# Last group of the SSM stage: which projections are products of parts, and where the rests of x are taken

## The chip, the cores and the metric

One core of a Trainium2 chip. The metric is the device time of one launch in microseconds (us). The engines are TensorE (PE, with its weight loads as PEld), VectorE (DVE), ScalarE (ACT), GpSimd (POOL) and SyncE (SP, which only issues transfers here).

## The reference, cut to what matters

The kernel is one step of a hybrid decoder layer on 544 tokens (512 of a prompt and 32 of eight samples). All branches begin with one projection of x:

```
cq, ckv_raw, kr_raw, z, xbc, dt_raw, mq, g_raw = split(x @ w_in)
# branch B (SSM), four groups of 8 heads of 64, chunks of 128 tokens
xbc -> causal conv -> silu -> xs, B, C
per chunk:  w = (C.B) * exp(cum_i - cum_j) * dt ;  y = w @ xs + (C @ S) * exp(cum)
            S = S * exp(last) + B^T (wb * xs)
y = (y + d_skip * xs) * silu(z) ; RMS norm over each group
# branch A (latent attention)
ckv = rms_norm(ckv_raw) ; krope = rope(kr_raw) ; q = rms_norm(cq) @ w_uq ...
```

A group of the SSM stage needs its 4 blocks of z (128 columns of w_in each) and computes, beside them, 6 blocks of something else: the conv inputs of the next group, or, in the last group, the latents (3 of cq, 2 of ckv, 1 of kr). These 6 are called "ahead".

## The kernel before, in words

Activations lie with features on the 128 partitions and the 544 tokens in the free dimension: x is 8 chunks (KC) of 128 features. A projection is one weight block of 128x1024 against x: for each half of the tokens (272 columns) 8 products, one for each chunk. There are two forms. The plain form (`project`, L1893) multiplies float32 by float32; the trace shows each such product as two records. The form of products of parts (`project_split`, L1908) multiplies rounded parts (type fp32r): x = XH + XL and w = high + low, and each chunk takes three products: high by XH, high by XL, low by XH. So a plain projection has 32 records and a split one 48.

The parts come from other engines. ACT rounds a weight block into one of three buffers (`round_head_block`, L774), DVE subtracts and leaves the rest in the block's own ring slot (`rest_of_head_block`, L1395, tile `ring_parts`). ACT rounds x into XH in group 2 (L779); DVE takes the rests XL (`rest_of_chunks`, L1389, tile `x_low`). `x_low` lies where `xt` lies: a chunk's rest overwrites the chunk, so DVE may take it only when the last plain product has read that chunk (semaphore `x_read`).

The stage runs a loop over 4 groups, with each engine's order written out by hand. TensorE: `project_x(1)`; sums of the last group; transposes of x and B (`turn`); `project_x(0)`, `project_x(1)` with the B by C products within, `project_x(0)` with the chunk states within (L2124). These four are z. Then `read_out(0)` (L2141 and L2147, two heads), `project_x(1)` with `sample_off` (L2157) within, `read_out(1)`, and five more projections with the samples' products and `read_out(2)`, `read_out(3)` between. `read_out(h)` waits for the two decay tiles that DVE has weighed (`weigh`, L1458) and for C scaled by GpSimd (`scale_c`, L515). After `sample_off` GpSimd scales four blocks of the samples' states (L521), two more C, and four more blocks. The split projection waits for `split_ready` of its block.

In groups 0 to 2 all ten projections are plain, in group 3 all ten are split. At the end of group 2 DVE takes the eight rests of x and the rest of the first split block, and only then runs the conv of the last ahead block (L1328 to L1342). ACT rounds ten blocks: two in the end of group 2, eight in group 3. `round_head_block(i)` waits, for i of 3 and more, until the block that used the same buffer has been read (`blocks_begun`). The ring has four slots that SP fills in order.

Of the kernel before, what the change touches and what calls it, by code (L numbers as in the profile page):

```python
# [3 lines left out]
P = 128  # L4
# [174 lines left out]
def program(nc, stream, x_t, mem_t, const, vec, conv_state, ssm_state, pages, ckv_rows, page_cols,  # L179
# [7 lines left out]
    with ExitStack() as ctx:  # L187
# [539 lines left out]
        def _(act):  # L727
# [130 lines left out]
            for g in range(GROUPS):  # L858
# [35 lines left out]
                if last_group:  # L894
                    round_head_block(3)
                if g:
# [262 lines left out]
        def _(dve):  # L1159
# [254 lines left out]
            for g in range(GROUPS):  # L1414
# [8 lines left out]
                rest_in_last_group(1)  # L1423

                def turned(*cs):
# [34 lines left out]
                z_gate(0)  # L1460
                rest_in_last_group(2)
                turned(2, 3)
# [9 lines left out]
                z_gate(1)  # L1472
                rest_in_last_group(3)
                dve.wait_ge(sem["rows_s_loaded"], t.next("rows_s_loaded", 16))
# [20 lines left out]
                weigh(1)  # L1495
                rest_in_last_group(4)
                z_gate(2)
# [6 lines left out]
                weigh(3)  # L1504
                rest_in_last_group(5)

# [43 lines left out]
                weigh(5)  # L1550
                rest_in_last_group(6)
                read_y(1)
                rest_in_last_group(7)
                ahead(1, between=read_y_s)
# [8 lines left out]
                add_state(1)  # L1563
                rest_in_last_group(8)
                ahead(2)
# [5 lines left out]
                gate_y(2)  # L1571
                rest_in_last_group(9)
                add_state(4)
# [9 lines left out]
                ahead_finish(3)  # L1583
                if g == GROUPS - 2:
                    for c in range(KC):
                        if c < KC - 1:
                            dve.wait_ge(sem["x_read"], c + 1)
                        else:
                            dve.wait_ge(sem["acc0_ready"], 4 + 5 * (GROUPS - 1))
# [283 lines left out]
        def _(pe):  # L1873
# [8 lines left out]

            def project(p, x, n_blocks=1, width=HT, between=None, read=None):

                pe.wait_ge(sem[f"acc{p}_free"], t.next(f"acc{p}_free"))
                for b in range(n_blocks):
                    w = next_block()
                    for half in range(2):
                        if half and between:
                            between()  # L1890
                        for k in range(KC):
                            kk = b * KC + k
                            m = pe.matmul(acc[p][:, half, 0:width], w[:, k * P:(k + 1) * P],  # L1893
                                          x(kk)[:, half * width:(half + 1) * width],
                                          start=kk == 0, stop=kk == n_blocks * KC - 1)
                            if half == 0 and k == 0:
                                m.then_inc(sem["blocks_begun"], 1)
                            elif half and read and k < KC - 1:
                                m.then_inc(sem[read], 1)
                m.then_inc(sem[f"acc{p}_ready"], 1)  # L1900
# [171 lines left out]
            for g in range(GROUPS):  # L2072
                B, C_ = bc[g % 2][:, 0, :], bc[g % 2][:, 1, :]
                def project_x(p, between=None, first=False, last=False):
                    if g == GROUPS - 1:
                        project_split(p, between, "low_even" if first else None)
                    else:
                        project(p, of_x, between=between, read="x_read" if last and g == GROUPS - 2 else None)

                project_x(1, first=True)  # L2080
                if g:
# [34 lines left out]

                project_x(1, between=b_by_c)
                pe.wait_ge(sem["b_tm_read"], t.next("b_tm_read"))
# [8 lines left out]
                states(0, 1)  # L2127
                project_x(0, between=lambda: states(2, 3))

# [55 lines left out]
                read_out(0)  # L2185
                project_x(1, between=sample_off)
                read_out(1)
                project_x(0)
                sample_y()
                project_x(1, between=lambda: state_adds(0))  # L2190
                read_out(2)
                state_adds(2)
                project_x(0, between=lambda: state_adds(4))
                read_out(3)
                project_x(1, between=lambda: state_adds(6))
                project_x(0, last=True)

# [431 lines left out]
```

## Time and profile before

| | |
|---|---|
| median of 3 runs | 1671.23 us (1668.9 to 1674.76) |
| profiled execution, its own time | 1669.8 us |
| its span | 1668.1 us |
| mean granted clock | 0.99 |
| PE busy | 1612.6 us, 97% |
| PEld busy | 1410.7 us, 85% |
| DVE busy | 797.4 us, 48% |
| ACT busy | 463.4 us, 28% |
| POOL busy | 411.1 us, 25% |

All times in the profile are from the span's start. A row of a timeline is: start, length, engine, line, operation, output tile and input tiles, their shapes, how many like it were merged, and in brackets the idle time before it with what ended it. Matmuls overlap in the records, so the pace is the distance of starts, not the length.

### The profile page before, as it was taken

The numbers are of one execution on the slowest core, as the hardware profiler recorded it, in microseconds if no ns is written. First come the engines' busy times: TensorE is split into PE (matmuls) and PEld (weight loads), VectorE is DVE, ScalarE is ACT, GpSimd is POOL, SyncE is SP. The second block draws the span as 40 slices with busy tenths as digits, with TensorE's granted clock in tenths as the row PEclk, the third lists the DMA queues.
The fourth block names the chain that finished last, engine by engine and source line by source line (L and its number), as shares of the span: only waits on it lengthen the run. The fifth ranks groups of instructions, "written<-read, shape, count | busy, mean of one in ns | idle before, by whom it ended". The sixth has DMA issues, their size and how long they took to land.

```text
span 1668.1 us, 27396 instructions
## 1 busy us (share of the span) xinstructions
PE 1612.6 (97%) x11110; PEld 1410.7 (85%) x11110; DVE 797.4 (48%) x1360; ACT 463.4 (28%) x867; POOL 411.1 (25%) x344
## 2 busy tenths in 40 slices
PE   8999999989999999999999999999989999999995
PEld 6878787768988888888888877789978999999995
DVE  5658676677533222223333223254488751177234
ACT  2252433526432222222122111142234111111122
POOL 0041131403320000001244200124444333344432
PEclk9999999999999999999999999999999999999998
DMA  5424334243462222224788766423322233222211
GB/s 179 136 81 165 95 110 144 76 155 108 140 231 66 74 76 76 64 78 152 254 270 270 250 260 245 160 89 89 102 64 64 89 89 89 89 89 84 86 59 54
DMA packets 71857, 210.67 MB, mean 126 GB/s; under 512 B 10321, under 2 KB 26962, under 8 KB 66866
## 3 DMA queue, kind: packets, MB, share of 16 engines
q1 hardware_dynamic: 51968, 157.04, 29.7%
q10 hardware_dynamic: 13618, 30.89, 5.2%
q0 software_dynamic: 6144, 20.98, 3.5%
q8 instruction: 88, 1.44, 0.4%
q14 instruction: 39, 0.32, 0.1%
HBM read 194.01 MB, written 14.86 MB: 125 GB/s over the span
## 4 chain that ended last, share of the span: by engine, by line
PE 82%; DVE 9%; ACTq 3%; ACT 3%; issue 2%; DMA 1%; SPq 0%; POOL 0%; DVEq 0%
PE acc L1962 30%; PE acc L1893 16%; PE acc L1908 12%; PE acc L2274 4%; PE acc L2237 3%; PE acc L2220 2%; ACTq L1053 1%; ACTq L1051 1%; DVE work L1342 1%; PE bank L2288 1%; PE bank L2307 1%; PE bank L2289 1%; DVE ring_parts L1395 1%; PE bank L2360 1%; PE bank L2392 1%
## 5 line engine op out<-in xcount | busy, mean ns | idle before, releaser
L1893 PE MATMUL acc<-xt,ring 128*128 128x272 f32 x1184 | 282.3, 395 | 0.0
L1893 PEld LDWEIGHTS acc<-xt,ring 128*128 128x128 f32 x1184 | 222.3, 190 | 53.1 <-issue 9.3
L1962 PE MATMUL acc<-x_parts,f_parts 128*128 128x272 f32 x1408 | 219.6, 291 | 10.6 <-DVE x_parts L1269 6.1
L565 POOL TENSOR_TENSOR f_parts<-ring,f_parts 128x1024 fp32r<-128x1024 f32 x65 | 157.9, 2429 | 247.9 <-ACT f_parts L789 247.6
L1962 PEld LDWEIGHTS acc<-x_parts,f_parts 128*128 128x128 f32 x1408 | 196.0, 191 | 13.3 <-issue 6.0
L543 POOL DMA_DIRECT2D work<-in_page_cols x128 | 68.9, 539 | 420.7 <-PE bank L2328 383.9
L1962 PE MATMUL acc<-f_parts 128*128 128x272 f32 x1344 | 172.3, 289 | 0.0
L1962 PEld LDWEIGHTS acc<-f_parts 128*128 128x128 f32 x1344 | 170.4, 188 | 0.1
L1908 PE MATMUL acc<-x_low,high 128*128 128x272 f32 x480 | 138.0, 288 | 0.0
L1908 PE MATMUL acc<-work_high,ring_parts 128*128 128x272 f32 x468 | 135.6, 290 | 0.0
L789 ACT ACTIVATE f_parts<-ring 128x1024 fp32r<-128x1024 f32 x65 | 69.0, 1061 | 238.9 <-PE acc L1962 204.5
L1908 PE MATMUL acc<-work_high,high 128*128 128x272 f32 x428 | 124.5, 291 | 0.0
L1395 DVE TENSOR_TENSOR ring_parts<-ring,high 128x1024 fp32r<-128x1024 f32 x38 | 48.4, 1274 | 90.4 <-ACT high L774 90.1
L1908 PEld LDWEIGHTS acc<-x_low,high 128*128 128x128 f32 x480 | 90.9, 189 | 0.4 <-issue 0.2
L1908 PEld LDWEIGHTS acc<-work_high,ring_parts 128*128 128x128 f32 x468 | 89.5, 191 | 0.0
L1908 PEld LDWEIGHTS acc<-work_high,high 128*128 128x128 f32 x428 | 80.4, 188 | 0.0
L1856 DVE TENSOR_SCALAR f_parts<-attended 128x544 fp32r<-128x544 f32 x32 | 76.2, 2383 | 1.1
L1342 DVE SCALAR_TENSOR_TENSOR work<-work,vecs 128x600 f32<-128x600 f32 x72 | 68.5, 951 | 2.4
L1962 PE MATMUL acc<-f_parts,mg_parts 128*128 128x272 f32 x528 | 68.8, 289 | 0.0
L565 POOL TENSOR_TENSOR mg_parts<-ring,mg_parts 128x1024 fp32r<-128x1024 f32 x21 | 50.8, 2417 | 71.1 <-ACT mg_parts L789 71.1
L1962 PEld LDWEIGHTS acc<-f_parts,mg_parts 128*128 128x128 f32 x528 | 67.3, 188 | 0.2
L1962 PE MATMUL acc<-x_parts,mg_parts 128*128 128x272 f32 x480 | 62.1, 289 | 0.6 <-DVE attended L1850 0.6
(385 smaller groups left out, 2738.7 us busy)
## 6 DMA issues: line engine op xcount, KB each, us to landing
ring<-in_stream SPq DMA_DIRECT2D x216, 512.0 KB, 3.6
work<-in_page_cols POOLq DMA_DIRECT2D x128, 160.0 KB, 5.2
attended<-in_ssm_state ACTq DMA_DIRECT2D x8, 1024.0 KB, 7.0
work<-cum_rows SPq DMA_DIRECT2D x32, 256.0 KB, 4.5
out_ssm_s<-attended ACTq DMA_DIRECT2D x8, 1024.0 KB, 5.7
work<-in_ckv_rows ACTq DMA_DIRECT2D x64, 128.0 KB, 3.6
work<-in_ckv_rows SPq DMA_DIRECT2D x64, 128.0 KB, 2.7
work<-in_memk_cols SPq DMA_DIRECT2D x8, 1024.0 KB, 7.1
```

The source lines that it names most:

```text
L543: pool.dma_start(keys[kq][:, i * KEYS_W:(i + 1) * KEYS_W], page_cols[ids[kq * 4 + i]]).then_inc(sem[f"keys_in_slot{kq}"], 16)
L565: pool.tensor_tensor(lo, ring[:, s * BLOCK:(s + 1) * BLOCK], hi.bitcast(F), SUB).then_inc(sem["split_ready"], 1)
L789: act.activation(hi, ring[:, s * BLOCK:(s + 1) * BLOCK], ACT.Copy).then_inc(sem["hi_ready"], 1)
L1342: dve.scalar_tensor_tensor(out=c, in0=ext[j][:, i:i + CL], scalar=tap(i), in1=c, op0=MUL, op1=ADD).then_inc(sem[signal], 1)
L1395: dve.tensor_tensor(ring_parts[:, of], ring[:, of], w_high_of(i).bitcast(F), SUB).then_inc(sem["split_ready"], 1)
L1856: dve.tensor_scalar(hi, q, 1.0, None, MUL).then_inc(sem["dve_step"], 1)
L1893: m = pe.matmul(acc[p][:, half, 0:width], w[:, k * P:(k + 1) * P], x(kk)[:, half * width:(half + 1) * width], start=kk == 0, stop=kk == n_ ...
L1908: m = pe.matmul(out[:, half, 0:HT], w[:, k * P:(k + 1) * P], x[k][:, of], start=k == 0 and n == 0, stop=last and k == KC - 1 and n == 2)
L1962: m = pe.matmul(acc_half, w[:, k * P:(k + 1) * P], x[:, kk, of], start=kk == 0 and n == 0, stop=kk == last and n == 2)
L2220: m = pe.matmul(acc[p][:, 0, 0:N_MEM], w[:, k * P:(k + 1) * P], mem[:, k, :], start=k == 0, stop=k == KC - 1)
L2237: m = pe.matmul(acc[p][:, half, 0:HT], w[:, c * 256 + off:c * 256 + off + P], cq[:, c, half * HT:(half + 1) * HT], start=c == 0, stop=c == 2)
L2274: m = pe.matmul(acc[1][:, half, 0:HT], w[:, k * P:(k + 1) * P], BR[:, KC + k, half * HT:(half + 1) * HT], start=False, stop=k == KC - 1)
```

## The change

In group 3 the four z projections become plain; the six latent ones stay split. The blocks that ACT and DVE split are numbered from the first latent block, so four rounds and four rests of weight blocks go. The fourth z projection runs chunk by chunk, both halves of a chunk together, and frees each chunk of x as it goes. DVE takes the eight rests of x in group 3, after `weigh(3)`. The first latent projection runs its products with XH first (two for each chunk, both halves, `sample_off` between), and then, chunk by chunk behind DVE, its products with XL. The end of group 2 has no rests and no rounds of weight blocks left.

```diff
-GROUP_SPLIT = GC + QC
+GROUP_SPLIT = QC
 # ACT, group 3
-                    round_head_block(2)          # after silu(0)
-                    round_head_block(3)          # after z_read(0)
                 z_read(1)
-                    round_head_block(4)
+                    round_head_block(0)
                 z_read(2)
-                    round_head_block(5)
+                    round_head_block(1)
                 ...
                 z_read(3)
-                    round_head_block(6)
+                    round_head_block(2)
                 # ahead(q)
-                    if g == GROUPS - 2 and q in (3, 4):
-                        round_head_block(q - 3)
-                        round_head_block(7 + q)
+                        round_head_block(3 + q)
 # DVE, group 3 (rest_in_last_group 1, 2, 3 before: gone)
                 weigh(0)
                 weigh(1)
-                rest_in_last_group(4)
+                rest_in_last_group(0)
                 ...
                 weigh(2)
                 weigh(3)
-                rest_in_last_group(5)
+                if g == GROUPS - 1:
+                    for c in range(KC):
+                        if c < KC - 1:
+                            dve.wait_ge(sem["x_read"], c + 1)
+                        else:
+                            dve.wait_ge(sem["acc0_ready"], 4 + 5 * (GROUPS - 1) + 2)
+                        rest_of_chunks(XL, X, XH, (c,))
+                rest_in_last_group(1)
 # (later ones: 6, 7, 8, 9 become 2, 3, 4, 5 at the same places)
 # DVE, end of group 2
-                if g == GROUPS - 2:
-                    for c in range(KC):
-                        ...
-                        rest_of_chunks(XL, X, XH, (c,))
-                    rest_of_head_block(0)
                 ahead(5)
 # PE
+            def project_by_chunk(p, between):
+                ...
+                for k in range(KC):
+                    if k == KC // 2:
+                        between()
+                    for half, of in enumerate(halves):
+                        m = pe.matmul(acc[p][:, half, 0:HT], w[:, k * P:(k + 1) * P], X[:, k, of],
+                                      start=k == 0, stop=k == KC - 1)
+                        if half:
+                            m.then_inc(sem["x_read" if k < KC - 1 else f"acc{p}_ready"], 1)
+            def project_low_last(p, between):
+                ...
+                w_high, w_low = next_split_block()
+                for half, of in enumerate(halves):
+                    for k in range(KC):
+                        for w in (w_high, w_low):
+                            m = pe.matmul(acc[p][:, half, 0:HT], w[:, k * P:(k + 1) * P], XH[k][:, of], ...)
+                    if half == 0:
+                        between()
+                for k in range(KC):
+                    pe.wait_ge(sem["low_even"], t.next("low_even"))
+                    for half, of in enumerate(halves):
+                        m = pe.matmul(acc[p][:, half, 0:HT], w_high[:, k * P:(k + 1) * P], XL[k][:, of], ...)
+                m.then_inc(sem[f"acc{p}_ready"], 1)
-                project_x(1, first=True)
+                project(1, of_x)
-                project_x(0, between=lambda: turn(2, 3))
+                project(0, of_x, between=lambda: turn(2, 3))
-                project_x(1, between=b_by_c)
+                project(1, of_x, between=b_by_c)
-                project_x(0, between=lambda: states(2, 3))
+                if g == GROUPS - 1:
+                    project_by_chunk(0, lambda: states(2, 3))
+                else:
+                    project(0, of_x, between=lambda: states(2, 3))
                 read_out(0)
-                project_x(1, between=sample_off)
+                if g == GROUPS - 1:
+                    project_low_last(1, sample_off)
+                else:
+                    project(1, of_x, between=sample_off)
                 read_out(1)
                 # the five after it: project_ahead, split in group 3 and plain before, as they were
```

## Rows read from the trace of the kernel before

**Rows 1.** Waits of TensorE, whole span, first of them: total us, times, longest us.
```profile
PE acc L1908 <- DVE ring_parts L1395: 6.4, 2, 6.2
```
**Rows 2.** Timeline of TensorE where group 2 ends and group 3 begins.
```profile
363.54 0.56 PE L1908 MATMUL acc<-high,work_high 128*128 128x272 f32 x1 [6.16 <-DVE ring_parts L1395]
...
372.21 1.08 PE L2068 MATMUL bank<-work,cst 128*128 128x272 f32 x4
...
387.87 0.40 PE L1908 MATMUL acc<-high 128*128 128x272 f32 x1
...
391.01 1.88 PE L2124 MATMUL bank<-work 128*128 128x512 f32 x4
```
**Rows 3.** Timeline of VectorE there: the first rests of x, the block's rest, the conv.
```profile
357.12 1.36 DVE L1389 TENSOR_TENSOR x_low<-xt,high 128x544 fp32r<-128x544 f32 x2
...
362.21 1.22 DVE L1395 TENSOR_TENSOR ring_parts<-ring,work_high 128x1024 fp32r<-128x1024 f32 x1
363.35 0.17 DVE L1328 TENSOR_SCALAR work<-work 128x24 f32<-128x24 f32 x1
```
**Rows 4.** Timeline of ScalarE: it empties the group's last accumulator, before group 2 and 3.
```profile
258.04 0.62 ACT L805 ACTIVATE work<-acc 128x544 f32<-128x544 f32 x1 [0.41 <-PE acc L1893]
...
357.41 0.62 ACT L805 ACTIVATE work<-acc 128x544 f32<-128x544 f32 x1 [0.41 <-PE acc L1893]
```
**Rows 5.** Timeline of TensorE in group 2: readouts, and plain projections between them.
```profile
297.77 0.66 PE L2141 MATMUL bank<-work 128*64 128x128 f32 x8 [0.57 <-DVE work L1458]
...
299.45 3.94 PE L1893 MATMUL acc<-xt,ring 128*128 128x272 f32 x16
303.31 1.93 PE L2157 MATMUL bank<-attended,work 128*32 128x512 f32 x16
305.17 3.93 PE L1893 MATMUL acc<-xt,ring 128*128 128x272 f32 x16
...
310.72 7.60 PE L1893 MATMUL acc<-xt,ring 128*128 128x272 f32 x32
318.16 0.30 PE L2165 MATMUL bank<-cst,work 128*128 128x32 f32 x2
```
**Rows 6.** Timeline of TensorE in group 3: first and second readout.
```profile
402.07 0.66 PE L2141 MATMUL bank<-work 128*64 128x128 f32 x8 [1.15 <-DVE work L1458]
...
412.07 0.66 PE L2141 MATMUL bank<-work 128*64 128x128 f32 x8
```
**Rows 7.** Timeline of VectorE: the fourth weighed decay of group 2, and what follows.
```profile
302.53 0.69 DVE L1458 TENSOR_TENSOR work<-work 128x512 f32<-128x512 f32 x1 [1.55 <-ACT work L885]
303.14 0.74 DVE L1513 SCALAR_TENSOR_TENSOR branch<-branch,vecs,bank 128x512 f32<-128x512 f32 x1
```
**Rows 8.** One line's instructions, shortest, median and longest in ns: L521, L1395, L774.
```profile
L521 POOL TENSOR_TENSOR attended<-attended,work x32: 1035/1044/2023, 109.0 to 426.4; 128x512 f32<-128x512 f32 x32
L1395 DVE TENSOR_TENSOR ring_parts<-ring,work_high x4: 1206/1218/2026, 362.2 to 435.6; 128x1024 fp32r<-128x1024 f32 x4
L774 ACT ACTIVATE work_high<-ring x4: 1057/1062/1064, 342.1 to 431.8; 128x1024 fp32r<-128x1024 f32 x4
```
**Rows 9.** Timeline of group 3 where VectorE and GpSimd work side by side.
```profile
409.82 1.10 POOL L515 TENSOR_TENSOR work<-work 128x384 f32<-128x384 f32 x1 [1.14 <-ACT work L886]
409.97 2.04 DVE L1395 TENSOR_TENSOR ring_parts<-ring,high 128x1024 fp32r<-128x1024 f32 x1
...
426.89 2.95 DVE L1458 TENSOR_TENSOR work<-work 128x512 f32<-128x512 f32 x2
```
**Rows 10.** Stretches: busy us (count) of PE, PEld, DVE, ACT, POOL; clock; DMA; GB/s.
```profile
361.00:362.00 1.00, 0.00 (x0) 0.00 (x0) 1.00 (x3) 0.00 (x0) 0.00 (x0) 1.00 1.00 418
368.00:369.00 1.00, 1.00 (x6) 1.00 (x6) 0.61 (x2) 0.64 (x1) 0.25 (x1) 0.50 0.67 267
1250.00:1252.00 2.00, 0.37 (x1) 0.37 (x2) 1.97 (x4) 1.40 (x3) 1.57 (x2) 0.50 0.00 0
1254.00:1256.00 2.00, 2.00 (x10) 1.75 (x8) 1.97 (x2) 0.32 (x1) 1.44 (x1) 0.50 0.00 0
```

More of the change, by code:

```diff
@@ L1421, in rest_in_last_group @@
                         rest_of_head_block(i)
-                rest_in_last_group(1)
                 def turned(*cs):
@@ L1460, in _ @@
                 z_gate(0)
-                rest_in_last_group(2)
                 turned(2, 3)
@@ L1472, in _ @@
                 z_gate(1)
-                rest_in_last_group(3)
                 dve.wait_ge(sem["rows_s_loaded"], t.next("rows_s_loaded", 16))
@@ L1550, in _ @@
                 weigh(5)
-                rest_in_last_group(6)
+                rest_in_last_group(2)
                 read_y(1)
-                rest_in_last_group(7)
+                rest_in_last_group(3)
                 ahead(1, between=read_y_s)
@@ L1563, in _ @@
                 add_state(1)
-                rest_in_last_group(8)
+                rest_in_last_group(4)
                 ahead(2)
@@ L1571, in _ @@
                 gate_y(2)
-                rest_in_last_group(9)
+                rest_in_last_group(5)
                 add_state(4)
@@ L1881, in next_block, with project @@
                 return ring[:, s * BLOCK:(s + 1) * BLOCK]
-            def project(p, x, n_blocks=1, width=HT, between=None, read=None):
+            def project_by_chunk(p, between):
+                pe.wait_ge(sem[f"acc{p}_free"], t.next(f"acc{p}_free"))
+                w = next_block()
+                for k in range(KC):
[4 more added lines that the diff above has]
+                                      start=k == 0, stop=k == KC - 1)
+                        if half == 0 and k == 0:
+                            m.then_inc(sem["blocks_begun"], 1)
+                        if half:
+                            m.then_inc(sem["x_read" if k < KC - 1 else f"acc{p}_ready"], 1)
+            def project_low_last(p, between):
+                pe.wait_ge(sem[f"acc{p}_free"], t.next(f"acc{p}_free"))
+                w_high, w_low = next_split_block()
+                for half, of in enumerate(halves):
+                    for k in range(KC):
+                        for w in (w_high, w_low):
+                            m = pe.matmul(acc[p][:, half, 0:HT], w[:, k * P:(k + 1) * P], XH[k][:, of],
+                                          start=k == 0 and w is w_high, stop=False)
+                            if half == 0 and k == 0 and w is w_high:
+                                m.then_inc(sem["blocks_begun"], 1)
+                    if half == 0:
[3 more added lines that the diff above has]
+                    for half, of in enumerate(halves):
+                        m = pe.matmul(acc[p][:, half, 0:HT], w_high[:, k * P:(k + 1) * P], XL[k][:, of],
+                                      start=False, stop=k == KC - 1)
+                m.then_inc(sem[f"acc{p}_ready"], 1)
+            def project(p, x, n_blocks=1, width=HT, between=None):
                 pe.wait_ge(sem[f"acc{p}_free"], t.next(f"acc{p}_free"))
@@ L1897, in project @@
                                 m.then_inc(sem["blocks_begun"], 1)
-                            elif half and read and k < KC - 1:
-                                m.then_inc(sem[read], 1)
                 m.then_inc(sem[f"acc{p}_ready"], 1)
@@ L2073, in _, with project_ahead @@
                 B, C_ = bc[g % 2][:, 0, :], bc[g % 2][:, 1, :]
-                def project_x(p, between=None, first=False, last=False):
+                def project_ahead(p, between=None):
                     if g == GROUPS - 1:
-                        project_split(p, between, "low_even" if first else None)
+                        project_split(p, between)
                     else:
-                        project(p, of_x, between=between, read="x_read" if last and g == GROUPS - 2 else None)
-                project_x(1, first=True)
+                        project(p, of_x, between=between)
+                project(1, of_x)
                 if g:
@@ L2185, in _ @@
                 read_out(0)
-                project_x(1, between=sample_off)
+                if g == GROUPS - 1:
+                    project_low_last(1, sample_off)
+                else:
+                    project(1, of_x, between=sample_off)
                 read_out(1)
-                project_x(0)
+                project_ahead(0)
                 sample_y()
-                project_x(1, between=lambda: state_adds(0))
+                project_ahead(1, between=lambda: state_adds(0))
                 read_out(2)
                 state_adds(2)
-                project_x(0, between=lambda: state_adds(4))
+                project_ahead(0, between=lambda: state_adds(4))
                 read_out(3)
-                project_x(1, between=lambda: state_adds(6))
-                project_x(0, last=True)
+                project_ahead(1, between=lambda: state_adds(6))
+                project_ahead(0)
             pe.wait_ge(sem["squares_ready"], t.next("squares_ready", 3))
```

5 lines of the change are left out of this document (removed).

## The prediction

> **What bounds the kernel now.** The page's first part says that TensorE is busy for 97% of the span, so a change pays only where it shortens TensorE's own work, ends one of its waits, or gives it its clock back. I read the waits of TensorE next. Their longest is the first split projection of group 3, which stood for the rest of its weight block: 6.2 us at one place [rows 1]. The timeline of TensorE shows that place at 357.4 to 363.54 [rows 2], and that of VectorE shows what went on: eight rests of x and one rest of a weight block in a row [rows 3]. The stretches show a second loss. The granted clock is still 1.00 at 361, while TensorE stands, and 0.50 at 368, in dense work [rows 10]: TensorE fell to 1.2 GHz behind the idle stretch and worked there for some 5.6 us. The split projection that begins at 363.54 took 8.67 us to the next work [rows 2].
>
> **The prices of the two forms.** A split projection at 2.4 GHz is two halves of 24 products. One half runs from 387.87 to 391.01, that is 3.14 us, so 6.28 us in all [rows 2]. One whole plain projection, 16 products of two records each, runs from 310.72 to 318.16 [rows 5]: 7.44 us. A plain one is thus dearer by 7.44 - 6.28 = 1.16 us, and four of them by 4.6 us. Against that stand 6.2 us of wait and 8.67 - 6.28 = 2.4 us of low clock.
>
> **Step 1: from the end of group 2 to read_out(0).** After the change this stretch is, for TensorE and nearly so for VectorE, what group 2 runs already: plain projections, no rest between. So its length can be read off. ScalarE empties the last accumulator of the group ahead at 258.04 for group 2 and at 357.41 for group 3 [rows 4]: the shift between the groups is 99.37 us. Group 2 began its read_out(0) at 297.77 [rows 5], so group 3 should at 297.77 + 99.37 = 397.14. It did at 402.07 [rows 6]. That is 4.9 us earlier. The sum of parts agrees: 6.2 + 2.4, less 4.6, and 1.15 - 0.57 = 0.6 of a smaller wait for the weighed decay [rows 5, 6] give 4.6. Taking the fourth projection chunk by chunk changes the order of 16 products and not their number; I price it at nothing, with a bound of 0.3 us on either side. Of ScalarE's rounds, two now stand between its reads of z and its decays. Group 2's decays were ready before VectorE came to weigh them, so they are covered there; uncovered they would cost one round, 1.06 us [rows 8]. The conv that stood behind the rests of x starts earlier by what they took, and TensorE's transposes, which wait for it, come 7.4 us after group 3 begins. SP's loads follow the blocks that TensorE begins, and a slot is filled three projections ahead: nothing.
>
> **Step 2: from read_out(0) to read_out(1).** Here the new wait stands. The first latent projection issues 32 products with XH, and they need the block's rest, which VectorE takes right after weigh(1), as before. At 3.14/24 = 0.13 us each they take 4.2 us; read_out(0) takes 299.45 - 297.77 = 1.7 us and sample_off 305.17 - 303.31 = 1.9 us [rows 5]. TensorE is through at 397.14 + 7.8 = 404.9 and needs XL from there. VectorE starts XL only after weigh(3). In group 2 weigh(3) ended at 303.14 [rows 7], and everything ahead of it hangs on ScalarE, whose fourth read of z ends with the fourth projection. ScalarE now has a round between this read and decays(2): 1.06 us [rows 8]. So weigh(3) ends at 303.14 + 1.06 + 99.37 = 403.6. Eight rests of x took 362.21 - 357.12 = 5.1 us when GpSimd was quiet [rows 3]. It is not quiet here: its fourth scaling of C comes as weigh(3) ends (409.82, beside a rest that begins at 409.97 [rows 9]) and four scalings of the samples' states follow it.
>
> How much they cost is the open number. A rest of a block takes 1218 ns at the median and 2026 at most, a state scaling 1044 and 2023 [rows 8]; two weighs, 0.69 us each alone [rows 7], took 2.95 beside GpSimd [rows 9]. Each longest is a median and about one operation of the other engine. I read that as turns: one waits for the other to finish, and the other for it. Five GpSimd operations lie in VectorE's way, four at a hold of 0.95 us (a little under the 1.035 of a whole one [rows 8]) and the first alike: 4.8 us. Then XL is done at 403.6 + 5.1 + 4.8 = 413.5, and TensorE's last two products and the step between the engines bring the next work to 413.7. Before it was 412.07 [rows 6]. Bounds: without any effect of GpSimd 408.9, with each of the five at the full 1.10 of a scaling of C [rows 9] 414.4. By these the two steps together give between -3.2 and +2.3 us; I take +1.6.
>
> The Trainium skill (SBUF — State Buffer, section "SBUF: two separate sides") says that a VectorE operation with two SBUF inputs and a GpSimd operation that reads SBUF hold a shared port pair exclusively, the loser blocked until the end. By it the five would add their whole length. If the rows were instead a sharing of bandwidth, with a rest stretched 2026/1218 = 1.66 times while GpSimd is active, XL would take some 8.1 us in place of 9.9 and the sum would be -0.2 us. The trace's longest values, each a median plus an operation of the other side, fit the lock better.
>
> **Step 3: the clock.** From 404.9 to 413.7 TensorE has 16 products, 2.1 us of work in 8.8. The trace has no stretch that is starved like this. Nearest are the idle 6.2 us above, after which the clock was at half, and a stretch at 1250 where the work came thinly and the clock was at half as well, and stayed so through the first dense work at 1254 [rows 10]. If it falls here, read_out(1) and most of the next projection run at 1.2 GHz, and the price is that of the same thing before: 2.4 us. Bounds: 0, and 4.3 us, worked out under the third rival. I take 2.4.
>
> The Trainium skill (TensorE: Matmul & The Clock Gate, section "A second HAM failure mode: psum-queue depth-cycling") tells of a kernel whose TensorE idles briefly but often between groups of matmuls and loses its clock for it, though no single gap is long. By that the fall belongs in the sum; by a reading that only one long gap counts it would not.
>
> **Step 4: the rest of the group.** Past read_out(1) the order is that of before. VectorE's rest of the second latent block ends 1.2 us after XL, inside read_out(1)'s 1.7. read_y(0) begins later against TensorE than it did, by some 2 us; before, VectorE then sat idle for several us until decays(4), which hang on ScalarE and so on TensorE's own end. Nothing later waited. I carry the shift to the end unchanged.
>
> **The sum.** -4.9 + 6.5 (10.0 us between the two readouts before, 16.5 now) + 2.4 = +4.0 us. On the profiled execution, 1669.8 us of its own (span 1668.1), that is 1673.8. The median of the runs shown is 1671.2, 1.4 above it, so the forecast for the median is 1675.2 us. Differences under 0.3%, 5.0 us, can't be told from no change in this kernel.
>
> **The rivals.**
> First, the clock holds, since no gap between two chunks is longer than some 1.5 us. Then +1.6: 1672.8. For it speaks that at 361, after 4 us of full idleness, the clock still stood at 1.00 [rows 10]; against it the thin stretch at 1250.
> Second, GpSimd hardly gets into VectorE's way, since VectorE's rests stand ready one behind another and GpSimd's states start late. XL ends at 409 to 411, the starved stretch is shorter and the clock holds: -1 to -3.2, around 1669. For it speaks only that the rows of contention are few; against it that the longest values are that clear.
> Third, the other side, slower: the clock falls early in the starved stretch and stays down until dense work has gone on for a while, as at 1254, where it was still 0.50 in full work [rows 10]. If it stays at half from 413.7 to beyond the end of read_out(1) and the whole next projection, 1.7 + 6.3 = 8.0 us of work run at half speed for some 8 to 9 us and lose 4.3, and +5.9 gives 1677.1. It decides when the low clock outlasts 413.7 by more than 7 us.
> That the first step's gain fails (the wait at 357 only shrinks) I hold for unlikely: nothing but the rests stood behind it.
>
> **Chances.** The forecast 0.40, the clock that holds 0.27, little contention 0.18, the long low clock 0.15. Range: from 1668.5, which takes in most of the second rival, to 1678.5, for the third and the upper bound of XL. Slower by over 0.3%, above 1676.2: most of the third rival and a tenth or two of the forecast, 0.20. Faster by over 0.3%, below 1666.2: no case reaches it but by the spread of the runs, 0.05. Within 0.3%: 0.75.
>
> **What would show it.** In the changed profile: no wait of TensorE at the start of group 3, and clock 1.00 there; read_out(0) 39.7 us after the accumulator is emptied (step 1). The rests of x behind weigh(3) in 9 to 10 us with GpSimd's state scalings between them, each near 1.5 us, and products with `x_low` in pairs that wait for them; read_out(1) some 16.5 us after read_out(0) (step 2). A clock of 0.50 around that place (step 3). The prediction is wrong if the rests of x take near 5 us, if a later wait of TensorE comes up in group 3 that was not there, or if read_out(0) is not some 5 us earlier.

## The result and the profile after

The changed kernel takes 1673.35 us (median of 18 runs, 1671.43 to 1676.69) against 1670.57 us before (18 runs, 1667.83 to 1674.76): a ratio of 1.0015, 95% interval 1.0008 to 1.0022. That is 1.3 to 3.7 us more, a slowing of under 0.3%, and 1.85 us less than the 1675.2 us forecast. The profiled execution has a span of 1672.7 us at a mean granted clock of 0.988; the one before had 1668.1.

First ScalarE and TensorE of the kernel after, in order of time: where the last accumulator of the group ahead is emptied (answers to [rows 4]), the plain projections of the new group (to [rows 2]), the first readout (to [rows 6]), the products with the rests of x, the second readout, the samples' products behind the next projection, and the end of the group. The first row is ScalarE's.

```profile
357.03 0.62 ACT L805 ACTIVATE work<-acc 128x544 f32<-128x544 f32 x1 [0.42 <-PE acc L1916]
354.76 9.56 PE L1916 MATMUL acc<-xt,ring 128*128 128x272 f32 x41
...
396.19 0.66 PE L2165 MATMUL bank<-work 128*64 128x128 f32 x8
404.68 0.52 PE L1902 MATMUL acc<-x_low,high 128*128 128x272 f32 x2 [0.43 <-DVE x_low L1384]
406.16 0.52 PE L1902 MATMUL acc<-x_low,high 128*128 128x272 f32 x2 [0.96 <-DVE x_low L1384]
...
410.62 2.72 PE L1902 MATMUL acc<-x_low,high 128*128 128x272 f32 x8 [0.97 <-DVE x_low L1384]
413.27 1.12 PE L2165 MATMUL bank<-work 128*64 128x128 f32 x8
...
422.69 0.30 PE L2189 MATMUL bank<-cst,work 128*128 128x32 f32 x2
...
455.20 2.92 PE L1954 MATMUL bank<-work,cst 128*128 128x272 f32 x12
```

The same last two places in the kernel before, same timeline:

```profile
419.93 0.31 PE L2165 MATMUL bank<-cst,work 128*128 128x32 f32 x2
...
452.42 2.92 PE L1933 MATMUL bank<-work,cst 128*128 128x272 f32 x12
```

TensorE runs through the start of the group without a gap, reads out 39.16 us after ScalarE's row (44.66 before), and then comes to products in pairs with nearly a microsecond of idleness ahead of each. From read_out(0) to the end of the group it takes 59.01 us; before it took 50.35.

The waits of TensorE (total us, times, longest): the 6.2 us of [rows 1] are gone, and this stands in their place.

```profile
PE acc L1902 <- DVE x_low L1384: 4.3, 5, 1.0
```

VectorE and GpSimd in that stretch, with the rests of x behind the fourth weighed decay and the four scalings of the samples' states beside them (answers to [rows 3, 7, 9]):

```profile
402.47 0.69 DVE L1451 TENSOR_TENSOR work<-work 128x512 f32<-128x512 f32 x1 [1.55 <-ACT work L885]
403.08 3.03 DVE L1384 TENSOR_TENSOR x_low<-xt,high 128x544 fp32r<-128x544 f32 x2
406.03 1.56 DVE L1384 TENSOR_TENSOR x_low<-xt,cst_high 128x544 fp32r<-128x544 f32 x1
407.51 4.95 DVE L1384 TENSOR_TENSOR x_low<-xt,work_high 128x544 fp32r<-128x544 f32 x5
412.39 1.21 DVE L1390 TENSOR_TENSOR ring_parts<-ring,high 128x1024 fp32r<-128x1024 f32 x1
402.93 1.11 POOL L515 TENSOR_TENSOR work<-work 128x384 f32<-128x384 f32 x1 [1.14 <-ACT work L886]
404.00 5.98 POOL L521 TENSOR_TENSOR attended<-attended,work 128x512 f32<-128x512 f32 x4
```

The eight rests take from 403.08 to 412.39, 9.3 us, where they took 5.1 at [rows 3]. Five lie one behind another at 1.5 us each beside GpSimd; the last ones, after GpSimd's end at 409.98, go at their own pace.

Stretches of the kernel after, columns as in [rows 10]:

```profile
360.00:362.50 2.50, 2.50 (x12) 2.07 (x11) 2.40 (x5) 0.70 (x1) 0.00 (x0) 1.00 0.98 400
...
407.50:410.00 2.50, 1.04 (x4) 0.59 (x4) 2.50 (x3) 0.00 (x0) 2.48 (x2) 0.97 0.00 0
410.00:412.50 2.50, 1.89 (x6) 1.50 (x6) 2.50 (x5) 0.00 (x0) 0.00 (x0) 0.50 0.00 0
412.50:415.00 2.50, 2.50 (x19) 2.23 (x20) 2.36 (x3) 1.28 (x2) 0.00 (x0) 0.50 0.00 0
415.00:417.50 2.50, 2.50 (x23) 2.17 (x20) 0.00 (x0) 0.53 (x1) 0.00 (x0) 0.67 0.03 7
```

The clock is 1.00 at the group's start now, and falls to half shortly before 410, after some 5 us in which TensorE had pairs of products with gaps. It comes back at 416.7, 6.8 us later (in the last stretch two thirds of 2.5 us are at half). read_out(1) to the samples' products takes 422.69 - 413.27 = 9.42 us, against 7.86 before: 1.6 us is what the low clock costs behind read_out(1).

### The profile page after: what moved, and what is told of

Its sections match the earlier page's. It is cut to its first block, busy times and chain, and to the rows that moved or that the text cites. A ratio compares the mean times of both kernels' runs of the same rounds, so it can differ in the third digit from the quotient of the medians.

```text
span 1672.7 us, 27256 instructions
## 1 busy us (share of the span) xinstructions
PE 1622.9 (97%) x11046; PEld 1414.5 (85%) x11046; DVE 795.7 (48%) x1356; ACT 459.3 (27%) x863; POOL 410.9 (25%) x344
## 4 chain that ended last, share of the span: by engine, by line
PE 83%; DVE 8%; ACT 3%; ACTq 3%; issue 2%; DMA 1%; SPq 0%; POOL 0%; DVEq 0%
PE acc L1983 30%; PE acc L1916 18%; PE acc L1929 10%; PE acc L2301 4%; PE acc L2264 3%; PE acc L2247 2%; ACTq L1048 1%; ACTq L1046 1%; PE bank L2315 1%; PE bank L2334 1%; PE bank L2316 1%; DVE work L1337 1%; PE bank L2387 1%; PE bank L2419 1%; PE bank L2282 1%
## 5 line engine op out<-in xcount | busy, mean ns | idle before, releaser
L1916 PE MATMUL acc<-xt,ring 128*128 128x272 f32 x1280 | 305.2, 395 | 0.0
L1916 PEld LDWEIGHTS acc<-xt,ring 128*128 128x128 f32 x1280 | 240.2, 190 | 57.0 <-issue 9.7
L789 ACT ACTIVATE f_parts<-ring 128x1024 fp32r<-128x1024 f32 x65 | 69.0, 1061 | 238.9 <-PE acc L1983 204.5
L1929 PE MATMUL acc<-x_low,high 128*128 128x272 f32 x432 | 124.2, 288 | 0.0
L1929 PE MATMUL acc<-work_high,ring_parts 128*128 128x272 f32 x418 | 120.5, 288 | 0.0
L1929 PE MATMUL acc<-work_high,high 128*128 128x272 f32 x398 | 115.8, 291 | 0.0
L1929 PEld LDWEIGHTS acc<-x_low,high 128*128 128x128 f32 x432 | 81.8, 189 | 0.4 <-issue 0.2
L1929 PEld LDWEIGHTS acc<-work_high,ring_parts 128*128 128x128 f32 x418 | 79.3, 190 | 0.0
L1929 PEld LDWEIGHTS acc<-work_high,high 128*128 128x128 f32 x398 | 74.8, 188 | 0.0
L1916 PE MATMUL acc<-attended,ring 128*128 128x272 f32 x256 | 63.3, 407 | 0.5 <-DVE attended L1756 0.5
```

What stands on the lines that cost most here:

```text
L789: act.activation(hi, ring[:, s * BLOCK:(s + 1) * BLOCK], ACT.Copy).then_inc(sem["hi_ready"], 1)
L1929: m = pe.matmul(out[:, half, 0:HT], w[:, k * P:(k + 1) * P], x[k][:, of], start=k == 0 and n == 0, stop=last and k == KC - 1 and n == 2)
```

## The experiments

Theory A is the account of the prediction with these numbers: what is lost behind read_out(0) is VectorE's rests held up by GpSimd (some 3.4 us) and, following from it, the clock (1.6 us), and the gain at the group's start is the wait and its clock. Theory B, the rival, looks for the loss in something else; each expectation says in what. Every ratio is to the kernel before, run beside the experiment on the same chip. The yardstick within a profile is the time from read_out(0) to the end of the group (50.35 us before, 59.01 after).

**Is it GpSimd?** GpSimd's four scalings of the states wait, in the last group, until all of x's rests are there. Every rest that VectorE takes adds one to `low_even`, and KC is 8.

```diff
                 pool.wait_ge(sem["s_off_ready"], t.next("s_off_ready"))
+                if g == GROUPS - 1:
+                    pool.wait_ge(sem["low_even"], KC)
                 for b in range(DEC_BATCH):
```

> Change against the changed kernel: in group 3 GpSimd begins its four state scalings (L521) only when all eight rests of x are taken. Theory A (VectorE and GpSimd take turns at SBUF, so four of the rests of x each wait for one whole state scaling): the eight rests shrink from 9.3 us to about 6 (5.1 us and one scaling of C), read_out(1) comes 3.5 to 4 us earlier against read_out(0), each rest near 0.64 us after the first. If the clock also holds, since TensorE is starved for 5 us and not for 9, another 1.6 us. In all 3.5 to 5.5 us less than the changed kernel, so about -1 to -3 us against the kernel before. Theory B (the rests are slow here for another reason, such as TensorE reading the same tiles): the rests stay near 9.3 us, the time stays within 1 us of the changed kernel's.

Measured: 1669.11 us, ratio to before 0.9989 (0.998 to 0.9998); the changed kernel stands at 1.0015, so this is some 4.3 us less. VectorE and GpSimd of this kernel, then TensorE's two readouts and its last product of the group:

```profile
403.67 2.18 DVE L1386 TENSOR_TENSOR x_low<-xt,high 128x544 fp32r<-128x544 f32 x2
405.76 0.71 DVE L1386 TENSOR_TENSOR x_low<-xt,cst_high 128x544 fp32r<-128x544 f32 x1
406.40 3.25 DVE L1386 TENSOR_TENSOR x_low<-xt,work_high 128x544 fp32r<-128x544 f32 x5
409.58 1.21 DVE L1392 TENSOR_TENSOR ring_parts<-ring,high 128x1024 fp32r<-128x1024 f32 x1
409.80 4.91 POOL L523 TENSOR_TENSOR attended<-attended,work 128x512 f32<-128x512 f32 x4 [5.18 <-DVE x_low L1386]
```

```profile
396.76 0.66 PE L2167 MATMUL bank<-work 128*64 128x128 f32 x8
...
410.15 0.66 PE L2167 MATMUL bank<-work 128*64 128x128 f32 x8
...
450.55 2.92 PE L1956 MATMUL bank<-work,cst 128*128 128x272 f32 x12
```

Eight rests now take 409.58 - 403.67 = 5.9 us; only the scaling of C at 403.51 still stands beside the first. TensorE's waits for them shrink from 4.3 us to one of 0.5, the clock stays at 1.00, and the time from read_out(0) to the group's end is 450.55 - 396.76 = 53.79 us, 5.2 less than after. read_out(1) now comes 13.4 us behind read_out(0). The contention, and what it drags along, is shown: the same rests without GpSimd beside them, and only one wait was added. The scalings begin 5 us later for it, and from the samples' products (418.02) to the group's end it takes 32.5 us as in the other kernels, so nothing behind them waits longer.

**The clock by itself.** Ahead of each of the first five waits for a rest TensorE does two products of constants into a bank that nobody reads.

```diff
                 for k in range(KC):
+                    for _ in range(2 if k < 5 else 0):
+                        pe.matmul(bank[3][:, 0:HT], C("ones"), C("rope")[:, 0:HT], start=True, stop=True)
                     pe.wait_ge(sem["low_even"], t.next("low_even"))
```

> Change against the changed kernel: before each of the first five waits for a rest of x TensorE runs two products of constants (float32, 272 columns, some 0.45 us each) into an idle PSUM bank; nothing reads them. Theory A (what the starved stretch costs beyond the wait is the low clock): the granted clock stays at 1.00, the rests of x and read_out(1) keep their places within 0.3 us, read_out(1) and the next projection take 7.9 us as in the kernel before and not 9.4, and the time falls by 1.6 us (1.2 to 2.4) against the changed kernel. Theory B (the clock falls by its own course, or its fall costs nothing at the end): no change within 0.5 us; or, if the added products are in the way of the low ones, up to 1 us more.

Measured: 1671.35 us, ratio 1.001 (1.0 to 1.002). The stretch from 404 to 408 has TensorE full and the clock up; the timeline of TensorE has read_out(1), the samples' products and the group's end so:

```profile
404.00:408.00 4.00, 3.95 (x20) 2.91 (x19) 4.00 (x4) 0.00 (x0) 4.00 (x3) 1.00 0.00 0
```

```profile
412.56 0.66 PE L2167 MATMUL bank<-work 128*64 128x128 f32 x8
...
420.43 0.31 PE L2191 MATMUL bank<-cst,work 128*128 128x32 f32 x2
...
452.92 2.92 PE L1956 MATMUL bank<-work,cst 128*128 128x272 f32 x12
```

The rests take the same 9.3 us. But read_out(1) to the samples' products is 7.87 us again instead of 9.42. The low clock had a second, smaller part ahead of read_out(1): with the clock up it begins 0.57 us after the last rest (412.56 - 411.99), with the low clock 0.88 (413.27 - 412.39). From read_out(0), at 395.78 here, to the end of the group it takes 57.14 us, so 1.9 us less than after: that is the whole price of the low clock here. The whole moved by 2.0 us in the medians and by 0.8 in the ratios, which here doesn't settle the size; the last experiment of this part comes back to it.

**The order of the chunks.** The fourth projection of the block ahead runs by halves again, as in the other groups, and only its reads of x are signalled.

```diff
 # project(..., read): the second half's products add to x_read, one for each chunk
-                if g == GROUPS - 1:
-                    project_by_chunk(0, lambda: states(2, 3))
-                else:
-                    project(0, of_x, between=lambda: states(2, 3))
+                project(0, of_x, between=lambda: states(2, 3), read=g == GROUPS - 1)
```

> Change against the changed kernel: the fourth z projection runs by halves again, as in the groups before, and frees the chunks of x in its second half. Theory A (freeing chunks early is worth nothing, since VectorE takes the rests only 6 us after that projection's end, behind weigh(3)): same time within 0.5 us, rests of x at the same place. Theory B (the chunk order lets the rests begin earlier): read_out(1) later by up to 2 us.

Measured: 1673.44 us, ratio 1.0011 (1.0001 to 1.002). read_out(0) is at 396.18 and read_out(1) at 413.26, within 0.01 us of after. This part of the change is worth nothing, as it was priced.

**What of the gain was clock.** The kernel before, with thirteen products of constants while TensorE stands for the block's rest at the start of group 3. The wait's length stays; only the idleness is filled.

```diff
+                if g == GROUPS - 1:
+                    pe.wait_ge(sem["acc1_free"], t.value("acc1_free") + 1)
+                    for _ in range(13):
+                        pe.matmul(acc[1][:, 0, 0:HT], C("ones"), C("rope")[:, 0:HT], start=True, stop=True)
                 project_x(1, first=True)
```

> Change against the kernel before: while TensorE waits at the start of group 3 it runs 13 products of constants into the accumulator that the split projection then overwrites. Theory A (the stretch at 1.2 GHz behind that wait cost 2.4 us): the clock stays at 1.00 there, the first split projection takes 6.3 us and not 8.7, and the time falls by 2 to 2.4 us against the kernel before, so that of the 4.9 us which the change gains ahead of read_out(0) half is clock. Theory B (the time lost to the clock is made up by waits that follow): less than 1 us.

Measured: 1666.89 us, ratio 0.998 (0.997 to 0.999): 3.3 us less than before by the ratio (1.7 to 5.0 by its interval), through thirteen products whose result is overwritten. TensorE and a stretch of it (answers to [rows 2, 10]):

```profile
356.46 6.12 PE L2083 MATMUL acc<-cst 128*128 128x272 f32 x26
362.78 0.36 PE L1908 MATMUL acc<-high,work_high 128*128 128x272 f32 x1 [0.20 <-issue]
...
398.78 0.66 PE L2145 MATMUL bank<-work 128*64 128x128 f32 x8 [1.15 <-DVE work L1458]
...
363.00:367.00 4.00, 4.00 (x33) 4.00 (x33) 3.86 (x6) 0.77 (x2) 0.00 (x0) 1.00 0.47 131
```

From ScalarE's row to read_out(0) it takes 398.78 - 356.66 = 42.12 us instead of 44.66: 2.5 us, the price of the low clock in that profile (8.67 against 6.15 us for the split projection). So of the 5.5 us that the change gains ahead of read_out(0) in the pair of profiles nearly half was clock, and it could be had without the change.

**A version without the loss?** TensorE does the XH products of both first blocks and read_out(1) between them, and takes the products with x's rests of both at the end; VectorE takes its rests of blocks and read_y(0) earlier, ScalarE decays(4) and (5) ahead of its round. Of the edit, TensorE's part:

```diff
-                    project_low_last(1, sample_off)
+                    w1 = high_part(1, sample_off)
+                    read_out(1)
+                    w0 = high_part(0)
+                    low_part(1, w1, True)
+                    low_part(0, w0, False)
```

> Change against the changed kernel: TensorE issues the products with XH of the first latent block, read_out(1), the products with XH of the second latent block, and only then the products with XL of both. VectorE takes the rest of the second latent block and the first readout's y in the gaps before weigh(2) and weigh(3), ScalarE computes decays(4) and (5) ahead of emptying the first latent. Theory A (the new wait is only a matter of what TensorE has to do meanwhile): the rests of x still take 9.3 us, but TensorE has 5.9 us more to do beside them, waits at most 1 us, keeps its clock, and the samples' products that now begin at 422.7 begin at about 415: 7 to 8 us less than the changed kernel, 4 to 6 us less than the one before. Theory B (VectorE is the bound of the whole group): the time comes back in later waits of TensorE on VectorE in group 3, and less than 3 us are gained on the changed kernel.

Measured: 1669.33 us, ratio 1.0003 (0.999 to 1.0016). From read_out(0) to the end of the group 450.75 - 395.89 = 54.86 us, 4.15 less than after, where theory A had promised 7 to 8. VectorE and GpSimd show why:

```profile
407.23 7.43 DVE L1387 TENSOR_TENSOR x_low<-xt,work_high 128x544 fp32r<-128x544 f32 x5
...
409.66 2.93 POOL L515 TENSOR_TENSOR work<-work 128x384 f32<-128x384 f32 x2
412.56 6.45 POOL L521 TENSOR_TENSOR attended<-attended,work 128x512 f32<-128x512 f32 x4
```

With decays(4) and (5) earlier, GpSimd's next scalings come straight behind its first four, and VectorE has them beside all eight rests: 11.8 us for them (from 402.79). TensorE catches up, waits 2.5 us for rests and loses its clock at 415. I had moved the other engine's work without counting where it would land. The twelve runs lie in two groups, eight from 1666.6 to 1670.0 us and four from 1673.6 to 1676.1; the four have a mean granted clock of 0.986 or 0.987, the eight of 0.989 to 0.992.

**Both.** The same with the wait of GpSimd from the first experiment.

> The kernel v1_lows_later with GpSimd's four state scalings held until the rests of x are taken. If TensorE has no wait left at the rests in v1, this adds nothing (within 0.5 us); if a wait of some 1 us is left there, it goes. Against it: the scalings move 5 us later and may get into the way of VectorE's later rests, at most +1 us.

Measured: 1663.17 us (1662.84 to 1663.79, five runs), ratio 0.9958 (0.9945 to 0.9971): 7.0 us faster than before and faster than both kernels. I had expected no more than 1 us over the version without the wait; it was 6 in the medians, of which 54.86 - 50.04 = 4.8 lie in this stretch; the rest can be the low clock of the other kernel's upper four runs. It was run in one set only. TensorE of this kernel:

```profile
404.56 0.66 PE L2177 MATMUL bank<-work 128*64 128x128 f32 x8
...
410.40 3.79 PE L1914 MATMUL acc<-x_low,high 128*128 128x272 f32 x29
...
446.58 2.92 PE L1966 MATMUL bank<-work,cst 128*128 128x272 f32 x12
```

No wait for a rest is left, the rests take 409.37 - 403.45 = 5.9 us, the clock is 1.00 from 396 to 426, and read_out(0) to the end takes 50.04 us, 9.0 less than after and as little as before, with step 1's gain kept.

**What belongs to an execution and what to the kernel.** One difference of the first pair of profiles lies far behind the change, in code that is the same in both: a fall of the clock. Stretches of the kernel after, and of the kernel before:

```profile
986.00:990.00 4.00, 3.48 (x14) 2.81 (x14) 2.12 (x9) 0.00 (x0) 0.00 (x0) 0.59 1.01 426
990.00:994.00 4.00, 4.00 (x11) 3.06 (x10) 0.00 (x0) 0.00 (x0) 0.00 (x0) 0.56 1.00 419
```

```profile
986.00:990.00 4.00, 4.00 (x19) 3.30 (x18) 0.80 (x4) 0.00 (x0) 0.00 (x0) 1.00 1.02 422
```

So four kernels ran once more, unaltered, in one set of runs, on another chip than the experiments above.

> The changed kernel once more, unaltered, beside the two below. The profiled execution before showed the clock at 0.59 in 986 to 990, in the dense mixture-of-experts work far behind the change, where the kernel before had 1.00. If that fall belongs to the program (its instructions or their placement), it comes again within a few us of the same place and the span is 1672 to 1673. If it is the phase at which an execution meets the clock's control (theory C: chance of the execution), it is gone or elsewhere in this execution, and the span moves by some 1.8 us. Median expected 1673.4, as before.

> The kernel before once more, unaltered, with a profile: the same question from the other side. By the program, the clock stays 1.00 in 982 to 994 and the span is 1668; by chance of the execution, a fall may stand there. The wait of 6.2 us at 357 and the half clock to 369 come again by both. Median expected 1670.6.

> The kernel with filled waits once more, now in the same set of runs as the changed one. By theory A (the low clock at 413 cost 1.6 us) its median lies 1.6 us under the changed kernel's; if the difference is under 0.5 us, the clock gained at 413 is lost elsewhere.

> The version with the products of x's rests of both blocks taken together, once more: its runs lay in two groups, 1666.6 to 1670 and 1673.6 to 1676. By chance of the execution the two groups come again, and the profile shows the clock's falls at other places than the first time; if the program fixes them, the median is 1669 and the profile is the same.

Measured, in this order: 1673.66, 1670.08, 1672.02 and 1670.33 us, ratios to before 1.0019 (1.001 to 1.0028), 0.9995, 1.0005 and 0.9995. The fall near 986 was absent from the changed kernel this time, and stood at 980 in the last one, which had not shown it the first time:

```profile
982.00:986.00 4.00, 4.00 (x25) 3.59 (x24) 1.71 (x6) 1.02 (x4) 0.00 (x0) 1.00 0.64 262
986.00:990.00 4.00, 3.48 (x28) 3.28 (x28) 1.41 (x8) 1.02 (x4) 0.00 (x0) 1.00 0.90 320
```

It is a matter of the execution, not of the change; of the twelve profiles kept here six have it within a few us of that place, one of them of a kernel built on the one before. What it costs can be read off one projection. The same 32 records, with the fall in the first execution of the changed kernel and without it in the second:

```profile
987.62 10.50 PE L1916 MATMUL acc<-attended,ring 128*128 128x272 f32 x32 [0.52 <-DVE attended L1756]
```

```profile
989.23 7.60 PE L1916 MATMUL acc<-attended,ring 128*128 128x272 f32 x32 [0.52 <-DVE attended L1756]
```

That is 2.9 us. The chip isn't needed to explain it: of the 32 runs of the kernel before in the first set of experiments, all on one chip, 15 have a mean granted clock of 0.986 to 0.988 and a median of 1672.3 us, the other 17 a clock of 0.989 or more and 1669.2 us. That the lower clock of each such run is this fall is a reading, since only profiled executions show its place.

The falls that do belong to the kernel, behind the wait at 357 and at 410, came again in both, yet not at the same instant: in the changed kernel the stretch 407.5 to 410 was at 0.97 the first time and at 0.50 the second, and read_out(1) to the samples' products took 423.45 - 413.77 = 9.68 us. There the low clock lasted until 417.7, over 3 us longer, and cost only 0.3 us more in this place: most of what was added lay ahead of read_out(1), where TensorE waited. In the kernel before the half clock lasted from about 360 to 367 instead of from 362 to 369, and ScalarE's row to read_out(0) took 400.53 - 356.35 = 44.18 us instead of 44.66. The filled kernel is 1.64 us under the changed one in this set by the medians and 2.3 by the ratios, and 2.02 from read_out(0) to the group's end in the profiles: the 1.6 that theory A names fits all of these. The intervals of the two ratios overlap, so it is the profiles that carry the size. The second set of the version with late rests lies between 1667.3 and 1673.7, and its profile has one fall more than the first, the one at 980; there the same projection took 10.1 us (983.01 to 993.14) against 7.4 (984.00 to 991.44). That fits the two groups of its first set, which may be executions with and without such a fall.

## Why the prediction was right, and where it was off

The forecast was no change that can be told, on the slow side: +4.0 us. Measured +2.8 and, in the second set, +3.4 (1673.66 against 1670.28). By its steps:

**Step 1, -4.9 us.** Measured 39.16 us from ScalarE's row to read_out(0) in both profiles of the changed kernel, against 44.66 and 44.18 before: -5.5 and -5.0. The wait is gone, the clock is up and the plain projections are dearer, as reckoned. The value read off group 2 (39.73) was 0.57 too high, the length of the wait for the weighed decay that group 2 has at [rows 5] and the changed group 3 has not: its row at 396.19 shows no idleness. The filling experiment separates the clock's part, 2.5 us for the 2.4 reckoned.

**Step 2, read_out(1) 16.5 us behind read_out(0).** Measured 17.1 in both. weigh(3) ended at 403.08 and not 403.6, XL at 412.39 and not 413.5; since TensorE was through read_out(0) a microsecond earlier than forecast, the distance still came out 0.6 longer. The term that carried the weight was five GpSimd operations at 0.95 us above the 5.1 of the rests: 9.9. Measured 9.3. The trace after has each rest under contention at 1.5 us, which is 0.64 and a hold of 0.85. Taking GpSimd's four states away gave 5.9. [Rows 8] already showed about that: 2026 - 1218 is 0.81 us, and 0.95 was taken.
The total came out nearer than its terms, which is luck: weigh(3) ended 6.9 us behind read_out(0) where 6.5 was reckoned, the rests took 0.6 less, and from the last rest to read_out(1) it took 0.88 us where 0.2 was allowed, 0.3 of it for the low clock.
The rival of a shared bandwidth, with 8.1 us for the rests, is refuted by the 9.3. Its sum of -0.2 us also left out step 3 without saying so; with the 2.4 it is +2.2.
The page "SBUF — State Buffer" of the Trainium skill (section "SBUF: two separate sides") has one side wait to the end of the other's operation. The runs bear out the turns: one rest per state scaling, at 1.5 us a turn on both engines; with GpSimd at work beside all eight rests they took 11.8 us, eight turns. A turn is 0.2 us shorter, though, than a rest (0.64) and a scaling (1.04 alone, [rows 8]) together; what part of an operation doesn't hold up the other was not tried.

**Step 3, the clock, +2.4 us.** The mechanism was right and the size too high. Behind read_out(1) the low clock cost 1.6 and 1.8 us in the two profiles; with the 0.3 ahead of it, the filling gives 1.9 and 2.0 in all. The term was sized after the other fall, where most of the low clock fell on dense work; here 2.5 of its 6.8 us went by before VectorE's last rest at 412.39, while TensorE had to wait in any case and half a clock costs nothing. That is the mis-sized term. The rival in which the clock holds is refuted, and so is the long low clock: it ended at 416.7, 3.4 us behind the start of read_out(1) (3.9 in the second profile), where the rival wanted over 7.
The page "TensorE: Matmul & The Clock Gate" (section "A second HAM failure mode: psum-queue depth-cycling"), again of the Trainium skill, says that brief and frequent idleness takes the clock too; no gap here was over 0.97 us, and it fell.

**Step 4, nothing else.** From the samples' products to the end of the group both kernels need 32.5 us (455.20 - 422.69 and 452.42 - 419.93). The shift is carried unchanged.

**The sum.** Steps 2 and 3 together were to cost 8.9 us; the profiles have 59.01 - 50.35 = 8.66, and 8.79 in the second pair. With step 1 that is +3.2 and +3.8. The profiled executions' spans differ by 4.6 and 4.8 us, but that hides chances of an execution: the second pair has a group 3 that began 1.2 us later (357.52 against 356.35), which closes it, and the first pair has the fall at 986, worth 2.9 us, and a group 3 that began 0.4 us earlier, which leaves 1.1 us of the other sign that was not followed. The medians agree with the steps. Of the 0.8 between +4.0 and +3.2, 0.6 is step 1; step 2 without its 0.3 of low clock came to 6.8 us, 0.3 over the forecast, and the clock's 1.9 are 0.5 under it. The 0.4 left to the +2.8 of the medians is within their interval. The medians need not be free of the fall at 986 either: a mean granted clock of 0.988 or less stands in 19 of 29 runs of the changed kernel and in 39 of 92 of the one before whose clocks are on record. If each of those runs has a fall worth some 3 us, that makes 0.7 us of the difference, an estimate from these counts; whether the change makes the fall more frequent was not tried. The time itself was 1.85 us too high, and 0.6 of that is the base: the runs shown before had a median of 1671.2, the 18 of the comparison 1670.57.

## What to carry to other kernels

Work that is moved off one wait lands beside another engine's: before moving a row of two-input VectorE operations, look at what GpSimd does in that place, and count one of its operations per VectorE operation. A wait on TensorE costs twice, by its length and by the clock behind it; products of constants whose result nobody reads take the second part away (in the kernel before 2.5 us of the profile, 3.3 of the time). The second part is small where TensorE would have waited on the low clock anyway. Where a moved step must meet another engine, hold that engine back with one wait and see whether it had slack; here the states could begin 5 us later with no new wait of TensorE, and with them behind the rests the late order went from no gain to 7 us.

## What had not been expected of the hardware

A fall of the clock starts and ends at other instants from one execution of a program to the next, and some falls come or stay away. Beside the place at 986, the stretch near 1250 that every kernel here has shows it: in two executions of the changed kernel it lasted until some 1267 and until some 1261. Stretches of the first, and of the second:

```profile
1252.00:1256.00 4.00, 1.70 (x6) 1.40 (x6) 3.55 (x6) 2.56 (x6) 4.00 (x5) 0.62 0.00 0
...
1264.00:1268.00 4.00, 4.00 (x23) 4.00 (x24) 2.32 (x7) 3.72 (x8) 1.53 (x2) 0.68 0.01 2
```

```profile
1260.00:1264.00 4.00, 2.69 (x18) 2.31 (x18) 3.75 (x9) 3.26 (x7) 0.94 (x2) 0.90 0.46 133
1264.00:1268.00 4.00, 3.36 (x25) 2.92 (x24) 2.29 (x6) 3.87 (x9) 1.65 (x3) 1.00 0.00 0
```

How long a fall lasts says little about its price. The one near 1250 lasted over 3 us longer in the first of these executions, and yet ScalarE's rounds on its two sides (L789) lie equally far apart: 1294.82 - 1237.06 = 57.76 us and 1293.45 - 1235.74 = 57.71. TensorE is busy for only 11 of the 17 us from 1250 to 1267 in the first, so the low clock had idle time to run in. The fall at 986, in a projection without gaps, cost 2.9 us. In this kernel a profile of one execution can therefore carry 3 us, as much as the change moves the medians, that no edit made. Which condition of an execution decides it was not tried.
